# The first expert's gate weights, given a place of their own and requested one stage earlier

## What is computed

```python
def trunk_layer(x, cond, lp, attend):
    ...
    x = x + gt1 * (merged @ lp['w_out'])
    h2 = rms_norm(x, lp['norm2_g']) * (1.0 + sc2) + sh2
    x = x + gt2 * hier_moe(h2, lp)
    return x, k, v

def hier_moe(h, lp):
    ...
    hid = jax.nn.silu(jnp.einsum('td,edf->tef', xt, lp['w_gate'])) * jnp.einsum('td,edf->tef', xt, lp['w_up'])
    hid = hid * combine[..., None].astype(hid.dtype)
    out = jnp.einsum('tef,efd->td', hid, lp['w_down'])
    return out.reshape(B, L, D)
```

## Time and profile before

| | us |
|---|---|
| runs before | 778.52, 776.72, 778.87 (median 778.52) |
| profiled execution, its own time | 778.7 |
| its span, first to last instruction | 777.0 |
| mixed stage and all before it, to the first transposes of expert rows | 445.1 |
| expert stage, to the start of the last expert's down products | 290.1 |
| the tail | 41.8 |

### The profile page before, as it was taken

How to read it: one execution, slowest core, us unless ns; L and a number is a source line. 1 busy time by engine, 2 the same in 40 slices (tenths; PEclk the granted TensorE clock), 3 DMA queues, 4 the chain that set the end, 5 groups by cost and what they waited for, 6 DMA issues and landing times. The chain is left out here.

```text
span 777.0 us, 10661 instructions
## 1 busy us (share of the span) xinstructions
PE 722.6 (93%) x3846; PEld 538.9 (69%) x3846; DVE 530.1 (68%) x811; ACT 402.8 (52%) x608; POOL 122.0 (16%) x165
## 2 busy tenths in 40 slices
PE   4899999899999989999999189999999999999995
PEld 1359998849999855555544168888888888888742
DVE  5355616369332025666657778999999999999828
ACT  1645433421233024545543376877887788878623
POOL 2000000000022017554211100121111111111100
PEclk9999999999999999999999689999999999999998
DMA  9992225113368558000003899999999999998555
GB/s 313 418 390 104 108 109 217 68 55 109 137 132 225 226 206 284 1 2 28 5 24 102 333 384 383 363 380 377 376 378 386 384 392 392 369 376 286 215 208 218
DMA packets 71793, 183.80 MB, mean 237 GB/s; under 512 B 9188, under 2 KB 9220, under 8 KB 68420
## 3 DMA queue, kind: packets, MB, share of 16 engines
q1 hardware_dynamic: 63252, 163.53, 57.0%
q0 software_dynamic: 6736, 17.51, 6.8%
q10 hardware_dynamic: 1760, 2.17, 0.9%
HBM read 175.30 MB, written 14.19 MB: 244 GB/s over the span
## 5 line engine op out<-in xcount | busy, mean ns | idle before, releaser
L1573 DVE TENSOR_TENSOR WL<-slot,WH 128x1024 fp32r<-128x1024 f32 x192 | 223.3, 1217 | 6.1 <-ACT WH L1080 5.4
L1080 ACT CAST WH<-slot 128x1024 fp32r<-128x1024 f32 x192 | 187.4, 1056 | 5.6 <-DMA slot<-in_w_gate 4.2
L1800 PE MATMUL bank<-WH,xgTh 128*128 128x512 f32 x256 | 102.6, 401 | 3.2 <-DVE xgTl L1565 1.8
L1800 PE MATMUL bank<-WL,xgTh 128*128 128x512 f32 x256 | 101.2, 395 | 0.0
L1800 PE MATMUL bank<-WH,xgTl 128*128 128x512 f32 x256 | 100.8, 394 | 0.0
L1800 PE MATMUL bank<-hTh,WP 128*128 128x384 f32 (+1 forms) x320 | 99.2, 310 | 0.6 <-DVE hTl L1233 0.6
L1800 PE MATMUL bank<-hTl,WP 128*128 128x384 f32 (+1 forms) x320 | 98.7, 308 | 0.0
L1800 PE MATMUL bank<-hTh,WL 128*128 128x384 f32 (+1 forms) x320 | 98.7, 308 | 0.0
L1702 PE MATMUL bank<-slot,big 128*128 128x512 f32 (+1 forms) x224 | 87.7, 539 | 0.1
L1711 PE MATMUL bank<-ident,big 128*128 128x128 f32 x424 | 61.4, 285 | 13.5 <-DMA big<-h_scratch,big 9.0
L522 DVE TENSOR_TENSOR WL<-slot,WP 128x1024 fp32r<-128x1024 f32 x24 | 29.3, 1233 | 62.7 <-ACT WP L516 62.1
(11 more groups left out here) (248 smaller groups left out, 1063.7 us busy)
## 6 DMA issues: line engine op xcount, KB each, us to landing
slot<-in_w_gate SPq DMA_DIRECT2D x16, 2048.0 KB, 14.4
slot<-in_w_up SPq DMA_DIRECT2D x16, 2048.0 KB, 15.7
slot<-in_w_down SPq DMA_DIRECT2D x16, 2048.0 KB, 15.6
slot<-in_w_ada SPq DMA_DIRECT2D x12, 2048.0 KB, 14.0
slot<-in_w_in SPq DMA_DIRECT2D x6, 2048.0 KB, 19.4
big<-y_scratch SPq DMA_DIRECT2D x10, 512.0 KB, 7.5
slot<-in_w_out SPq DMA_DIRECT2D x2, 2048.0 KB, 14.9
big<-m_scratch POOLq DMA_DIRECT2D x6, 512.0 KB, 8.6
```

Of the source, the lines that this page charges most:

```text
L1080: act.copy(WH[:, high_half(w, s), r, :], quarter(s, w, r)).then_inc(high_ok[w], 1)
L1573: dve.tensor_tensor(WL[ESLOT[3 * s + w]][:, r, :], quarter(s, w, r), WH[:, high_half(w, s), r, :].bitcast(F32), ALU.subtract).then_inc(low ...
L1800: ins = pe.matmul(out, l[u], r[v], start=first and i == 0, stop=last and i == 2)
```

## The change

The diff (without the line shifts) does four things. A buffer `first_gate` is placed at 106 KB to 122 KB of each partition, over the later part of `hyoT` and the value rows of the four latent tiles; `first_gate_low` is the same place under the type of the low parts. Expert 0's gate is loaded there instead of into slot 1. ACT, DVE and PE read it and write it there through `quarter` and `quarter_low`; the `isinstance` test leaves all other experts, and the second passes, as they were. And SP waits for `("o", 3)` and `("wh", 4, 1)` before this load; the wait for the last projection now stands between it and the load of up.

```diff
+        first_gate = part("first_gate", 106, [P, 4 * QW], F32)[:, :]
+        first_gate_low = part("first_gate_low", 106, [P, 4, QW])
...
-        def quarter(s, w, r):
+        def quarter(n, s, w, r):
-            return slot[ESLOT[3 * s + w]][:, r * QW:(r + 1) * QW]
+            home = first_gate if isinstance(n, int) and n + w == 0 else slot[ESLOT[3 * s + w]]
+            return home[:, r * QW:(r + 1) * QW]
+        def quarter_low(n, s, w, r):
+            return (first_gate_low if isinstance(n, int) and n + w == 0 else WL[ESLOT[3 * s + w]])[:, r, :]
...
-                sp.dma_start(slot[ESLOT[3 * s + j]].rearrange("p (k n) -> p k n", n=n), src)\
+                home = first_gate if isinstance(e, int) and e + j == 0 else slot[ESLOT[3 * s + j]]
+                sp.dma_start(home.rearrange("p (k n) -> p k n", n=n), src)\
...
+            full(sp, "o", NT - 2)
+            full(sp, "wh", NT - 1, 1)
+            load_weights(0, 0, 0)
             full(sp, *LAST_JOB[-1])
-            for j in range(2):
-                load_weights(j, 0, 0)
+            load_weights(1, 0, 0)
```

More of the change, by code:

```diff
@@ L1079, in high_parts @@
                         wait_past(act, freed, count + (r + 1))
-                    act.copy(WH[:, high_half(w, s), r, :], quarter(s, w, r)).then_inc(high_ok[w], 1)
+                    act.copy(WH[:, high_half(w, s), r, :], quarter(n, s, w, r)).then_inc(high_ok[w], 1)
             def rows_high(n):
@@ L1572, in low_parts @@
                     dve.wait_ge(high_ok[w], n * 4 + (r + 1))
-                    dve.tensor_tensor(WL[ESLOT[3 * s + w]][:, r, :], quarter(s, w, r),
+                    dve.tensor_tensor(quarter_low(n, s, w, r), quarter(n, s, w, r),
                                       WH[:, high_half(w, s), r, :].bitcast(F32), ALU.subtract).then_inc(low_ok[w], 1)
@@ L2080, in step @@
                             ins = products(bank[2 + w][:, :], (xgTh[:, 2 * r + k, :], xgTl[:, 2 * r + k, :]),
-                                           (WH[:, high_half(w, s), r, cols], WL[ESLOT[3 * s + w]][:, r, cols]),
+                                           (WH[:, high_half(w, s), r, cols], quarter_low(n, s, w, r)[:, cols]),
                                            r == 0 and k == 0, r == 3 and k == 1)
```

## The result

Twelve runs of each kernel gave 772.76 us (771.52 to 774.79) after the change and 777.21 us (774.11 to 780.02) before it. The ratio is 0.9947, with a 95% interval from 0.993 to 0.9964, or about 4.1 us (2.8 to 5.4). The forecast was 775.4, a gain of 3.1, with 773.4 as its lower end. The three runs that the forecast started from had a median of 778.52; with twelve the same kernel stands 1.3 us lower.

The account below looks back on a forecast made before the run. The prediction took PE to bound the kernel except at the join between mixed stage and experts. There 2.5 us (gather issued earlier) plus 0.6 (flight) gave 3.1 off the median 778.5, so 775.4 us, range 773.4 to 777.6.

Parts of the forecast that it names:

- the place: The join between mixed stage and experts, the one hole in PE's work, one tenth busy from 427 to 447 us.
- the chain: At the join, PE waits for the gather, the gather for the h2 store, the store behind gate and up.
- what is late next: At the join, once the store is early, DVE's index list, written at 435.48 us, releases the gather.
- The start: First gather at the join starts at 436.4 us instead of 438.9, 2.5 us earlier.
- The store: Last h2 store before the gather, behind one load instead of two, lands at 432.3 us instead of 438.0, 5.7 earlier.
- The early load: Expert 0's gate load, ahead of the join, leaves at 401.4 us instead of 422.35, at cost 0.
- the gather's flight: First gather at the join, issue to landing: 2.1 us issuing kept, 4.0 behind it falling to 3.4, gain 0.6.
- The quick gather: Rival at the join: rows land 2.35 us behind the issue, DVE becomes last, gain 4.1 us, 774.4; chance 0.17.
- The cap: At the join, DVE's routing ends at 442.76 us, so at most 4.1 us can come out of the gather.
- The clock: Rival behind PE's restart: one more half-clock stretch costs 1.7 us, giving 777.1; chance 0.18.
- the best case: At the join, the fastest gather landing, 774.4 us; the range's lower end is this less 1.0 us, 773.4.

Follow-up runs that it names:

- e11: Kernel before, with the last h2 store on POOL's queue and expert 0's down load moved behind the gathered rows and expert 1's gate; ratio 1.0027.
- e7: Kernel before, with three of four quarters of expert 0's gate low parts moved on VectorE behind the low parts of the first gathered rows; ratio 1.0.
- e6: Kernel before, with expert 0's down load moved behind the first gathered rows and expert 1's gate; ratio to before 1.0043.
- e2: Kernel before, with the last store of h2 issued by POOL on its own queue instead of by SP; ratio to before 1.0006.
- e5: Changed kernel, with an unused 1 MB filler load in the gate's old place in SP's list; ratio to before 0.999.
- e1: Changed kernel, with an unused 2 MB filler load in the gate's old place in SP's list; ratio to before 0.9999.
- e3: Changed kernel, with three of four quarters of expert 0's gate low parts moved on VectorE behind the gathered rows' low parts; ratio to before 0.9955.
- e8: Changed kernel, with ScalarE's copies of the early gate held until VectorE's assignment of tokens to experts; ratio to before 0.995.

## Why the prediction was right and where it was wrong

**Right: the place, the chain and what is late next.** The gate left at 399.87 and ACT's wait vanished for nothing; DVE's low parts stayed at +10.0; the gather's releaser became the index list. The start moved by 2.36 us (predicted 2.5). The store landed at +6.6 instead of +11.4, and 2.4 of these 4.8 us were lost to the list (predicted 3.2 of 5.7). It took 4.8 us from its issue (predicted 3.9), since up took 9.8 us and not the 8.7 of the gate that it replaced; the list covered that. The early load cost nothing that shows.

**Wrong: the gather's flight.** This is the step that failed: the term was 0.6 us in the sum, and 1.8 were measured (6.17 to 4.40). I had split the 6.1 us into 2.1 of issuing, which I carried over as a constant, and 4.0 behind it, for which I took 3.4. The second was right (3.33). The first fell to 1.07, which is most of what was missing. The two are not simply added, though. Four profiles give the flight with the issue long or short, and with down in flight or not:

| flight | down in flight | loads over |
|---|---|---|
| issue 2.0 to 2.1 | 6.2 (before) | 5.2 (e11) |
| issue 1.1 | 6.5 (e7) | 4.4 (the change, e6) |

In all nine profiles with the loads over, the rows came 3.1 to 3.6 us behind the end of the issue, and a shorter issue goes with a flight 0.8 us shorter. With down in flight a shorter issue was worth nothing (e7). So the change brought two things that pay together, and the prediction had only one of them. The right column compares kernels that differ in more than the issue, so its 0.8 us are read off and not tested by themselves. That the loads' end bounds the rows shows where it lies far behind the issue: in e2, e5 and e7 the rows came 2.2, 3.1 and 2.8 us behind the drained time, though the issue had ended 4.7, 1.1 and 2.6 us before it. In the kernel before, the issue's end (+14.4) and the drained time (+15.4) lie close together, and in e1 they are level, so these two alone could not tell. The rows of the kernel before had it: down landed at 443.8 and PE restarted at 445.1, and I read the load as company of the gather and not as its bound.

The quick gather, my first rival with a chance of 0.17, has the number that came, 4.13 us at the join against its 4.1, but by luck and not by its reason: it took 2.35 us behind an issue of 2.1 and let VectorE set the rest, where 3.33 behind 1.07 were measured and e3 shows that VectorE was not last. The Trainium skill ("DMA: Bandwidth & Descriptors", section on the anatomy of one DMA by the GpSimd path) would give such a transfer 3.2 us, an estimate from its fixed part and its rate. The traces do not agree: in e6_down_later, with idle DMA engines, it took 4.4, and in e2, with up and down beside it, 8.8.

**The cap** held. DVE was free at 441.15 and took up the rows at 441.27, 1.95 us behind the transposes.

**The clock** went both ways at once: its level rose later (half-clock products from 442.7 to 447.2, 4.5 us against 3.5 before) and the fall at 466 did not come. Net 1.16 us over the expert stretch in these two executions, 294.7 to 296.6 in all nine profiles without extra matmuls or moved weights. The fall at 145 to 180 adds a chance of the same size. The clock is not the whole of the spread, however: of the 35 executions of the kernel before beside e5 to e8, those with the same mean clock of 0.975 took from 775.33 to 780.41 us. What makes these differ stays open.

**The range** was missed by 0.6 us and the forecast by 2.6, by errors that add up: 1.0 us of the gain, 1.3 us in the starting point, which was a median of three runs, and 0.3 by which the medians differ more (4.45) than the ratio says (4.1). The range had been widened by half of their spread on one side of the best case, and that was too little for both.

Not tried: e11_both with the low parts moved as in e7, which would show by itself what the issue is worth once the loads are gone. While loads are in flight, the packets show that the gather's own bytes start late; why they do is not shown.

## What to carry to other kernels

Ask of a transfer on the critical path what else is in flight until it lands, on any queue, and not only what stands ahead of it in its own: bytes that are moved away from there pay twice, at the release and in flight, while moving only the release (e2) or only the issue (e7) paid nothing. Before a term is called worthless, ask what else bounds the same moment: the shorter issue was worth nothing beside a load, and without one it goes with 0.8 us less. An engine's wait for data that are loaded early is worth nothing as long as the next engine is busy (e8); the worth of an early load can be in what it no longer stands in front of. And take the starting time from enough runs: the median of three was 1.3 us off the median of twelve.

## What the runs showed of the hardware

POOL needed 1.0 to 1.1 us to issue a gather when VectorE was not in its 4.6 us run of low parts (line 1573), or when the gather began up to 0.1 us ahead of it. It needed 1.6 to 2.1 us in 14 of the 15 gathers, among the first two of each profile, that began within that run. The one case that speaks against a simple rule is the first gather of e6_down_later, which took 1.10 us. The cause stays open. With down in flight the longer issue cost nothing (e7); with the loads over it goes with a flight 0.8 us longer (e11).
